# Leftover rows of a pair of items turned by transposes of 64 rows into 64 columns instead of 128 by 128

## The reference

```
scores = sigmoid(xt @ w_router)                       # 1024 tokens, 64 experts
top_idx = top 8 of scores + bias; gates = top_s / sum(top_s) * 2.5
for each expert e and each of its tokens:
    routed[token] += gate * ((silu(x @ w_gate[e]) * (x @ w_up[e])) @ w_down[e])
h = h + routed + shared_expert(x)                     # inner width 256
```

## Time and profile before

| what | value |
|---|---|
| median of 3 runs | 1820.58 us (1817.6 to 1823.82) |
| profiled execution, its own time | 1818.86 us |
| its span, first to last instruction | 1817.0 us |
| mean granted TensorE clock | 0.957 |
| TensorE matmul busy (PE) | 1681.2 us, 93% of the span |
| TensorE weight load busy (PEld) | 1333.4 us, 73% |
| VectorE, ScalarE, GpSimd busy | 733.8, 627.7, 641.3 us |
| DMA | 348.68 MB, mean 192 GB/s; in the experts' loop about 320 GB/s |
| experts' loop | from about 862 to 1760 us of the span |

### The profile page before, as it was taken

The page is one execution under the profiler, slowest core; times in us unless marked ns, Lnnn a source line. Parts: engine busy times, 40 slices in busy tenths (PEclk is TensorE's granted clock), DMA queues, the critical chain, the costliest instruction groups (busy, mean ns, idle before and its releaser), DMA issues. The chain is left out here.

```text
span 1817.0 us, 29923 instructions
## 1 busy us (share of the span) xinstructions
PE 1681.2 (93%) x10076; PEld 1333.4 (73%) x10076; DVE 733.8 (40%) x1496; ACT 627.7 (35%) x997; POOL 641.3 (35%) x793
## 2 busy tenths in 40 slices
PE   4989899999997999996999999999999999999980
PEld 3767656555553456585989998999899989998970
DVE  5010266676765666542332333333333332323332
ACT  7111233333323232111334434443344344433433
POOL 1200000025652122331544544545455445554540
PEclk7989899999997999998999999999999999999995
DMA  4011100010007101144999999999999999999986
GB/s 141 1 47 35 35 24 23 23 35 23 23 12 273 41 24 47 47 164 145 299 322 322 318 318 315 320 329 306 323 324 316 315 323 313 330 304 323 330 243 221
DMA packets 111949, 348.68 MB, mean 192 GB/s; under 512 B 14591, under 2 KB 48064, under 8 KB 94510
## 3 DMA queue, kind: packets, MB, share of 16 engines
q1 hardware_dynamic: 78094, 260.23, 39.9%
q0 software_dynamic: 33824, 88.06, 20.1%
HBM read 290.46 MB, written 57.79 MB: 192 GB/s over the span
## 5 line engine op out<-in xcount | busy, mean ns | idle before, releaser
L1506 PE MATMUL gu<-XS,place 128*128 128x160 f32 x4224 | 596.5, 299 | 0.7 <-ACT XS L1585 0.7
L1506 PEld LDWEIGHTS gu<-XS,place 128*128 128x128 f32 x4224 | 583.8, 190 | 6.1 <-ACT XS L1585 1.1
L1641 DVE TENSOR_TENSOR WL<-place,WH 128x2048 fp32r<-128x2048 f32 x66 | 152.1, 2305 | 338.9 <-ACT WH L1577 338.9
L463 PE MATMUL bank<-xT,wi 128*128 128x512 f32 x512 | 239.9, 609 | 0.0
L1590 ACT ACTIVATE SS<-gu 128x160 f32<-128x160 f32 x132 | 40.1, 303 | 371.9 <-PE gu L1506 371.9
L463 PEld LDWEIGHTS bank<-xT,wi 128*128 128x128 f32 x512 | 93.3, 194 | 89.9 <-issue 89.9
L1646 DVE TENSOR_TENSOR SS<-SS,gu 128x160 f32<-128x160 f32 x132 | 41.7, 316 | 269.0 <-ACT SS L1590 269.0
L351 POOL TENSOR_TENSOR place<-place 128x514 f32<-128x514 f32 (+1 forms) x8 | 11.4, 1423 | 369.8 <-ACT place L533 369.5
L1600 ACT ACTIVATE YE<-ype,gta 128x512 f32<-128x512 f32 x132 | 90.8, 688 | 112.4 <-PE ype L1530 112.4
L1420 POOL DMA_INDIRECT acc_rows<-YF,sib x66 | 105.3, 1595 | 66.8 <-issue 32.7
L933 POOL DMA_INDIRECT slot_table<-pay,si x64 | 61.9, 968 | 187.3 <-DVEq L1205 170.2
(11 more groups left out here) (275 smaller groups left out, 2471.3 us busy)
## 6 DMA issues: line engine op xcount, KB each, us to landing
place<-in_w_gate_e SPq DMA_DIRECT2D x67, 1024.0 KB, 7.0
place<-in_w_up_e SPq DMA_DIRECT2D x67, 1024.0 KB, 9.7
place<-in_w_down_e SPq DMA_DIRECT2D x66, 1024.0 KB, 13.4
wi<-in_w_in SPq DMA_DIRECT2D x16, 512.0 KB, 4.0
xn_rows<-place SPq DMA_DIRECT2D x9, 512.0 KB, 2.6
xt<-in_x SPq DMA_DIRECT2D x8, 512.0 KB, 5.3
wbuf<-in_w_in SPq DMA_DIRECT2D x8, 512.0 KB, 4.2
wo<-in_w_out SPq DMA_DIRECT2D x2, 2048.0 KB, 10.2
```

Of the source, the lines that this page charges most:

```text
L463: last = pe.matmul(bank[blk][:, :], wbuf[s][:, t, :], K.xT[:, t, cols], start=(t == 0), stop=(t == KT - 1))
L1506: last = pe.matmul(gu[f][:, k, :], raw[:, t, f * P:f * P + P], XS[:, q, t, :], start=(t == 0), stop=(t == KT - 1))
L1641: tt(WL[q][:, :], WR[q][2][:, :], WH[q][:, :].bitcast(F32), ALU.subtract).then_inc(s_dlo, 1)
```

## The change

In `rest_turned` the eight transposes read only the 64 partitions of `XR` that hold rows, multiply by a 64 by 64 identity and write 64 columns of `xp`. In the loop TensorE gets a `sem_inc` on a new semaphore behind each of the two waits ahead of `rest_turned`. In `phase_out_route` the semaphore of the shared expert's down weights is given up: its load counts on `s_ws`, the first gate and up product waits for all three loads, and the wait before the first down product is gone.

```diff
@@ phase_out_route
-        s_w, s_ws, s_wd = sem("router_in"), sem("shared_in"), sem("shared_down_in")
+        s_w, s_ws = sem("router_in"), sem("shared_in")
...
-            sp.dma_start(wds[:, :, :], ins["w_down_s"].rearrange("l (f p) n -> p (l f) n", p=P)).then_inc(s_wd, 16)
+            sp.dma_start(wds[:, :, :], ins["w_down_s"].rearrange("l (f p) n -> p (l f) n", p=P)).then_inc(s_ws, 16)
...
                 if j == 0:
-                    pe.wait_ge(s_ws, 32)
+                    pe.wait_ge(s_ws, 48)
...
             def down(j):
-                if j == 0:
-                    pe.wait_ge(s_wd, 16)
                 pe.wait_ge(s_hs, j + 1)
@@ phase_experts
-        turn = {e: sem(f"turn_{e}") for e in ("sp", "pool")}
+        turn = {e: sem(f"turn_{e}") for e in ("sp", "pool", "pe")}
...
             def rest_turned():
 
-                rows = XR[:, :].rearrange("p (k t) -> p t k", t=KT)
+                rows = XR[0:2 * CAP1, :].rearrange("p (k t) -> p t k", t=KT)
                 for t in range(KT):
-                    last = pe.transpose(xp[t // 4][:, t % 4, :], rows[:, t, :], K.ident[:, :])
+                    last = pe.transpose(xp[t // 4][:, t % 4, 0:2 * CAP1], rows[:, t, :], K.ident[0:2 * CAP1, 0:2 * CAP1])
                 last.then_inc(s_tr, 1)
...
                 if ahead >= 2 and q == 0:
                     pe.wait_ge(s_gr, i * 16 + 32)
+                    pe.sem_inc(turn["pe"], 1)
                     pe.wait_ge(s_xk, n * 2 + 6)
+                    pe.sem_inc(turn["pe"], 1)
                     rest_turned()
```

## The result

| | before | after |
|---|---|---|
| median | 1820.18 us (22 runs, 1817.6 to 1823.82) | 1822.95 us (22 runs, 1820.03 to 1825.0) |
| ratio | | 1.0016, 95% interval 1.001 to 1.0022 |
| profiled execution: time, span, mean clock | 1818.86, 1817.0, 0.957 | 1821.38, 1819.6, 0.966 |

The change costs 2.8 us and saves nothing. The ratios in this document leave out one execution that was far slower than the rest of its kernel, 4462.88 us, in the variant with the old transposes and the new increments.

A forecast was written before the change was run, and what follows sets the result against it. TensorE, busy 100.00 of 100 us, was taken to bound the experts' loop and pace the DMA. 32 x (+0.09 - 0.055) less 0.1 gave +1.0 us on the 1820.58 median: 1821.6 us, range 1814 to 1828.

The forecast's parts named there:

- The load of 128 columns is the pace: Leftover-row transposes in the experts' loop: loading 128 stationary columns sets the 0.109 us per transpose, so 64 by 64 won't help.
- The way in: From gate and up to the leftover transposes: using 64 of 128 rows adds a switch, +0.09 us, bounds 0 and +0.10.
- The last stream: End of each transpose group, before the leftover product: half a stream saved, -0.055 us per group, bounds nothing or 0.11.
- Seven distances: Between the starts of the eight leftover transposes: 0.111 us each before, 0.110 after, so a change of 0.00 us.
- The sum: Whole kernel: 32 x (+0.09 - 0.055) = +1.1, less 0.1 for the first group, +1.0 us.
- the prediction's own signs: Changed profile: group about 1.0 us, loads 0.19, first load with its matmul, way in 4.44, last start to product 0.15.
- The increments: Two new semaphore increments per pair on TensorE's queue, 64 in all: 0 us, at most 0.01 each, 0.6 in all.
- the shared semaphore: Shared expert's down weights counting on the gate and up weights' semaphore: costs nothing, covered by 74 us.
- The first group: Leftover transposes ahead of the loop at clock 0.50: half a stream of about 0.2 us saved, 0.1 us less.
- Rival 1: Leftover transposes: streams, not loads, set the pace; each 0.055 us cheaper, 1809 us, or 1806 without switch and increments; chance 0.05.
- Rival 2: Leftover transposes: in a half-used array the next load isn't taken ahead; 20 us more, 1842 us; chance 0.05.
- Rival 3: TensorE's queue in the loop: an increment waits until the array is empty, 0.54 us each, 17 us, 1838; chance 0.03.

## Why the prediction was right, point by point

- *The load of 128 columns is the pace, and it stays.* Right at the full clock, and shown: 0.109 us from load to load after, 16 more transposes at 0.1125 us in the old shape, 8 more at 0.111 in the new one. Halving the stream bought nothing. The 0.104 read at L452 is a mean of unequal distances: in that trace the second start comes 0.055 us behind the first, and the others are 0.112 apart.
- *The way in, +0.09.* Right in kind: 0.10 measured to the first start, and it left with the shape (4.35) and not with an increment (4.44). To the first start a switch by rows costs what one by columns does. **But the term was too small, because that start is not the end of the switch.** The prediction read all its switches up to the first start behind them. With its load no longer taken ahead, the first matmul starts together with it, and the second comes 0.16 us later instead of 0.11. To the second start the switch costs (1315.27 - 1310.66) - (1313.81 - 1309.35) = 0.15, above the bound of 0.10.
- *The last stream, -0.055.* **This step failed.** From the last start to the leftover product there are 0.20 us before (1314.68 less 1314.48, which is 1313.70 + 1.05 - 0.27) and 0.20 after (the last start is 1315.11 + 1.09 - 0.27 = 1315.93). The product waits for something that does not shorten with the stream; what that is stays open. The term is 0, its bound of "nothing gained".
- *Seven distances, 0.00.* Right for six of them; the first is the 0.05 above. With 24 in a row the groups take 2.80 and 2.78 us, so it comes once per group and not per transpose.
- *The sum.* 0.15 to the second start, less 0.01 in the rest of the group, is the 0.14 of the pair shown. The mean of 31 pairs is 0.11: the products behind the group give 0.03 back, 1319.98 - 1316.13 = 3.85 to the next gate and up against 1318.56 - 1314.68 = 3.88. Why is open; the kernel with only the other order of storage has 3.85 too. 32 x 0.11 = 3.6 us where +1.1 was forecast. In time +2.8 (1.8 to 4.0) was measured, and the forecast was +1.0. That it held is owed to the range, 0.3% to either side, more than to the sum: the mechanism of the pace was right, and the gain that was to cancel most of the switch was not there. By the prediction's own signs, the 0.15 from the last start to the leftover product and the cancelling within 0.1 us a pair did not come; the group of 1.02 us, the loads of 0.20, the load that starts with its matmul and the 4.45 did.
- *The increments, 0; the shared semaphore, 0.* Right: with both in place and the old shape the loop is 892.51.
- *The first group, 0.1 less.* Wrong in size. At the half clock the streams set the pace and the load does not, so the group took 1.94 - 1.11 = 0.83 us less. I had argued from rows at the full clock alone. What is left of it is open. In this pair of profiles it was gone at the next group: gate and up took 851.23 - 844.47 = 6.76 us instead of 851.74 - 845.86 = 5.88, as the clock rose no earlier (at 848.8 before, at 849.2 after) and the work that came forward was done at the half clock; from the first tile's transposes to the second's it is 851.23 - 839.88 = 11.35 against 851.74 - 840.45 = 11.29. But that distance depends on when the clock rises in an execution: the old shape has 12.73 and 12.81 in two other profiles, the new one 11.89 and 10.78. A loss of 3.5 us in the loop and a gain of 0.8 ahead of it would make the 2.8 us measured; the profiles do not settle it.
- *Rival 1, the streams set the pace.* Refuted at the full clock, as said above.
- *Rival 2, no taking ahead in a half used array.* Refuted: 0.109 us from load to load on the same 64 rows. That is against the statement of the Trainium skill (TensorE: Matmul & The Clock Gate, The mechanism) that a load overlaps only where the row group differs; the same section also names a background weight buffer as a way to be taken ahead, and the trace does not contradict that.
- *Rival 3, an increment empties the array.* Refuted: 892.51 us for the loop with both increments, 892.53 without.

## What to carry to other kernels

At the full clock a float32 transpose in this kernel costs the load of its stationary operand, 0.11 us for 128 columns; fewer rows and a narrower identity did not make it cheaper, fewer loads did. So fill the 128 rows instead of trimming them: the version with two half rows stacked and one transpose for both took 1.1% off this kernel, two thirds of it in the loop. A shape that uses part of the array is a switch on the way in, here 0.15 us to the second transpose, and pays only if it saves more than that. Read a switch up to the second start behind it, not the first.

## What the runs showed that was not expected

- The granted clock can fall while TensorE has no gap at all: with 24 transposes of 64 rows into 64 columns in a row it fell to 0.50 for 3.4 us behind ten of the groups; with 24 of 128 by 128, or 16 of the small ones, it stayed at 1.00 in the loop of the one profile of each.
- It can rise while TensorE does nothing but large transposes. With the old shape three times over, TensorE turned the first full tile from 847.98 and then the 24, at clock 0.50; it was at 1.00 from 855.20, before the last of them ended.
- At the half clock the small transposes are nearly twice as fast as the large ones, 0.11 against 0.20 us, and at the full clock equal. A row measured at one clock doesn't tell which side binds at the other.
- The time of a stretch in which the clock rises says little from one profile: from the first tile's transposes to the second's it was 11.29, 12.73 and 12.81 us with the same transposes.
